# Second block's attention: two pipelines become one of 32 units, heads of the first kind taken in pairs, softmaxes mixed unscaled, and two chunks of the output projection moved beside it

## The chip, the cores and the metric

The kernel runs on one core of a Trainium2 chip. The metric is the device time of one execution in microseconds, from the program's start to its end on that core; lower is better.

## What is computed

`reference` runs two transformer blocks on 512 tokens of width 1024. The change touches only the attention of the second block. It has two kinds of heads. The first kind (`moba`) has 8 heads of width 64; with 512 tokens and blocks of 256 every query sees its own block and all earlier ones, so this is plain causal attention with a slope per head. The second kind (`diff`) has 4 heads with two query-key components of width 64 and values of width 128.

```
sc = q k^T * 64**-0.5 - slope * dist          # causal, both kinds
m_out = softmax(sc) v                          # first kind: 8 heads, v 64 wide
a = softmax(sc1) - lam * softmax(sc2)          # second kind: 4 heads
d_out = rms_norm(a v, diff_subln) * (1 - lambda_init)
mixed = concat(m_out * silu(mg), d_out * silu(dg))
x = x + mixed @ w_out
```

All of it is float32. The large products are made of three matmuls each, from a rounded high part and the low part that is left (`XAh`, `XAl` for the activations, `Rh`, `Rl` for the weights); the attention's own products are plain float32 matmuls.

## The kernel before

Everything is written by hand, engine by engine: five functions (`sync_program`, `tensor_program`, `scalar_program`, `gpsimd_program`, `vector_program`) issue each engine's instructions in order and wait on semaphores. `psum_plan` walks the same order and gives each use of one of the 8 PSUM banks its counts; `hold(tag)` waits until the bank's earlier use has been read. Weights come in 28 chunks of 128x1024 in the last part of the program (20 of `w_in2`, in groups `4, 5, 6, 3, 7` after the groups 0 to 2, and 8 of `w_out2`): SyncE loads one to `raw`, ScalarE writes its high part to a ring of five (`ahead`, L1079), GpSimd the low part (L1558), and TensorE runs 24 matmuls of 512 columns on it (`gemm_tok_chunk`, L652 to L654). This is called a chunk below.

`second_order` lays out the attention as a list of steps, `SECOND`, that every engine follows. A unit is one head and one block of 128 queries, which sees `nk` = 128, 256, 384 or 512 keys. For a unit, step A makes the scores (L1025), VectorE adds the slope (L2342), takes the maximum (L2346) and negates it (L2348), and ScalarE takes the exponential with its sum (L1508). Step B turns the softmax, `Pb`, with 1 to 4 transposes (L1037), which ScalarE copies to `PT2` (L1518). Step C multiplies it with v (L1054), and VectorE (L2359) or ScalarE (L1527) takes it to `mixed`. In a step n of the list C(n-3), B(n-2) and A(n) stand in a row, and then a piece of other work, `FILL_MOBA` or `FILL_DIFF`: chunks of the later projections, their norms (`norm2`), the transposes of q and k (`turn2`, L987), the gates.

The first kind is a pipeline of its own with 32 units, 36 steps and 12 chunks, the second another with 16 units, 19 steps that hold attention work and 8 chunks. A unit of the second kind has two halves of scores on two banks, and both softmaxes are scaled and added before the turning:

```
    own(e.tensor_scalar(p1, p1, s1[:, 3:4], None, ALU.mult))
    t = own(e.tensor_scalar(p2, p2, s2[:, 3:4], lam[:, 5:6], ALU.mult, ALU.mult))
    after(t)
    e.tensor_tensor(p1, p1, p2, ALU.add).then_inc(s["mixd"], 1)
```

After both pipelines follow the norm of the second kind's heads (L2385, with a square root by ScalarE), their gates (L2317), the 8 groups of four transposes of `mixed` (L1062), their high and low parts (L1540, L2392), the 8 chunks of the output projection, the addition of x (L2399) and the stores.

Of the kernel before, what the change touches and what calls it, by code (L numbers as in the profile page):

```python
# [94 lines left out]
for _m in range(NPARK):  # L95
    for _n in range(12):
        _k = 2 if 4 <= _n < 8 else 1
        if _m == NPARK // 2 and _n < 4:
# [7 lines left out]
FILL_MOBA = ([("proj", 4, 0), ("proj", 4, 1), ("proj", 4, 2), ("q2", 4, 2)]  # L106
             + [("proj", 5, 0, 2, 0), ("proj", 5, 1, 2, 1), ("proj", 5, 2, 2, 2), ("norm", 2, 3)]
             + [("turn", 2, k) for k in range(4)] + [("q2", 5, 3)]
             + [("proj", 6, 0, 3, 0), ("proj", 6, 1, 3, 1), ("proj", 6, 2, 3, 2), ("norm", 3, 3)]
             + [("turn", 3, k) for k in range(4)] + [("v2", 6, 1)])  # L110
FILL_DIFF = ([("proj", 3, 0), ("proj", 3, 1), ("proj", 3, 2), ("gate", 3, 0), ("gated", 0, 0), ("gated", 0, 2)]
             + [("proj", 7, 0), ("proj", 7, 1), ("proj", 7, 2), ("gate", 7, 1)])


def second_order():

    out = []
    for kind, units, fill, lag in (("m", 32, FILL_MOBA, 4), ("d", 16, FILL_DIFF, 7)):  # L120
        at = 0
        for n in range(units + lag):
            if kind == "d":
                for part in (2, 1, 0):
                    if n - 4 - part == 11 or (n - 4 - part == 15 and part < 2):
                        out.append(("dD", n - 4 - part, part))
            if 0 <= n - 3 < units:
                out.append((kind + "C", n - 3))
            if 0 <= n - 2 < units:
                out.append((kind + "B", n - 2))  # L130
            if n < units:
                out.append((kind + "A", n))
                steps = 22 if kind == "m" else 12
                take = (n + 1) * steps // units - n * steps // units
                out += fill[at:at + take]
                at += take
        out += fill[at:]
    return out
# [5 lines left out]
def psum_plan():  # L144
# [81 lines left out]
    n_ss = 0  # L226
    for step in SECOND:
# [6 lines left out]
        elif what in ("mA", "dA"):  # L234
            for i in range(1 if what == "mA" else 2):
                use(("ss", n_ss), n_ss % 2)
                n_ss += 1
        elif what in ("mB", "dB"):
            use(("tp", what[0], n), 2)
        elif what in ("mC", "dC"):  # L240
            use(("ap", what[0], n), 3)
    for k in range(8):
        use(("tm", k), (0, 1, 6, 7)[k % 4])
# [2250 lines left out]
```

## Time and profile before

| | us |
|---|---|
| median of 3 runs (lowest, highest) | 2395.33 (2394.08, 2401.38) |
| the profiled execution, its own time | 2386.53 |
| its span, first to last instruction | 2384.7 |
| TensorE busy in the span | 2175.2 (91%) |
| VectorE, GpSimd, ScalarE busy | 1780.5, 989.3, 944.7 |
| mean granted clock of TensorE | 0.951 |

The span is what the trace covers. A granted clock of 1.00 stands for TensorE's 2.4 GHz, 0.5 for its 1.2 GHz. The part that the change touches is the last 337 us of the span.

### The profile page before, as it was taken

The numbers are of one execution on the slowest core, as the hardware profiler recorded it, in microseconds if no ns is written. First come the engines' busy times: TensorE is split into PE (matmuls) and PEld (weight loads), VectorE is DVE, ScalarE is ACT, GpSimd is POOL, SyncE is SP. The second block draws the span as 40 slices with busy tenths as digits, with TensorE's granted clock in tenths as the row PEclk, the third lists the DMA queues.
The fourth block names the chain that finished last, engine by engine and source line by source line (L and its number), as shares of the span: only waits on it lengthen the run. The fifth ranks groups of instructions, "written<-read, shape, count | busy, mean of one in ns | idle before, by whom it ended". The sixth has DMA issues, their size and how long they took to land.

```text
span 2384.7 us, 29853 instructions
## 1 busy us (share of the span) xinstructions
PE 2175.2 (91%) x10645; PEld 1860.7 (78%) x10645; DVE 1780.5 (75%) x3593; ACT 944.7 (40%) x1543; POOL 989.3 (41%) x647
## 2 busy tenths in 40 slices
PE   3998899887899999899899999999999979998778
PEld 2786677666678999899788988889888867766557
DVE  7785887987553999999698788878888787444552
ACT  3335555434233444354333333333333343443441
POOL 2441122124353655699554345444444424311112
PEclk8999999998999999999999999999999999977779
DMA  7221111145542454366999999999999942211111
GB/s 292 76 89 59 57 58 63 63 158 176 194 168 81 162 167 149 119 238 240 328 362 370 347 335 342 357 338 358 333 345 361 340 161 102 71 36 36 36 36 45
DMA packets 176946, 455.84 MB, mean 191 GB/s; under 512 B 13600, under 2 KB 80544, under 8 KB 175136
## 3 DMA queue, kind: packets, MB, share of 16 engines
q1 hardware_dynamic: 136720, 293.55, 35.7%
q0 software_dynamic: 36864, 134.23, 15.0%
q10 hardware_dynamic: 3216, 26.15, 2.9%
q8 instruction: 86, 1.41, 0.2%
q14 instruction: 60, 0.49, 0.1%
HBM read 409.84 MB, written 44.04 MB: 190 GB/s over the span
## 4 chain that ended last, share of the span: by engine, by line
PE 63%; DVE 24%; ACT 4%; issue 2%; DMA 2%; POOL 0%; SPq 0%; ACTq 0%; DVEq 0%
PE bank L652 12%; PE bank L653 11%; PE bank L654 11%; PE bank L955 7%; PE bank L957 7%; PE bank L959 7%; DVE cout L1847 5%; DVE ohB L2130 4%; PE bank L1025 2%; DVE ohA L2129 2%; PE bank L1054 1%; DVE wk L2031 1%; DVE eqb L2081 1%; PE bank L1037 1%; DVE eqb L2077 1%
## 5 line engine op out<-in xcount | busy, mean ns | idle before, releaser
L1558 POOL TENSOR_TENSOR Rl<-raw,Rh 128x1024 fp32r<-128x1024 f32 x179 | 464.6, 2602 | 801.3 <-ACT Rh L1093 801.1
L652 PE MATMUL bank<-XAh,Rh 128*128 128x384 f32 (+1 forms) x1472 | 535.7, 364 | 37.2 <-POOL Rl L1558 15.4
L1093 ACT ACTIVATE Rh<-raw 128x1024 fp32r<-128x1024 f32 x380 | 399.6, 1056 | 352.6 <-DMA raw<-in_u 109.7
L653 PE MATMUL bank<-XAl,Rh 128*128 128x384 f32 (+1 forms) x1472 | 521.9, 355 | 0.0
L654 PE MATMUL bank<-XAh,Rl 128*128 128x384 f32 (+1 forms) x1472 | 521.8, 354 | 0.0
L652 PEld LDWEIGHTS bank<-XAh,Rh 128*128 128x128 f32 x1472 | 280.1, 190 | 60.5 <-issue 24.4
L653 PEld LDWEIGHTS bank<-XAl,Rh 128*128 128x128 f32 x1472 | 280.2, 190 | 18.3
L654 PEld LDWEIGHTS bank<-XAh,Rl 128*128 128x128 f32 x1472 | 279.5, 190 | 18.5
L1604 POOL DMA_INDIRECT ga<-in_v,eid x128 | 183.4, 1433 | 211.0 <-DVE y L2192 192.2
L1604 POOL DMA_INDIRECT ga<-in_un,eid x128 | 171.0, 1336 | 217.1 <-DVE act L2184 194.7
L955 PE MATMUL bank<-Rh,XGh 128*128 128x512 f32 x768 | 237.0, 390 | 2.6 <-issue 2.6
L957 PE MATMUL bank<-Rl,XGh 128*128 128x512 f32 x768 | 236.8, 389 | 0.0
L959 PE MATMUL bank<-Rh,XGl 128*128 128x512 f32 x768 | 236.7, 389 | 0.0
L2162 DVE TENSOR_TENSOR Rl<-raw,Rh 128x1024 fp32r<-128x1024 f32 x189 | 230.3, 1218 | 6.2 <-ACT Rh L1093 6.2
L1847 DVE SCALAR_TENSOR_TENSOR cout<-gb,vecs,cout 128x512 f32<-128x512 f32 x240 | 208.0, 866 | 2.1
L652 PE MATMUL bank<-Rh,XAh 128*128 128x512 f32 x416 | 172.2, 414 | 10.7 <-DVE XAl L1658 7.0
L2192 DVE SCALAR_TENSOR_TENSOR y<-ga,act,y 128x1024 f32<-128x1024 f32 x127 | 167.2, 1317 | 2.7
L955 PEld LDWEIGHTS bank<-Rh,XGh 128*128 128x128 f32 x768 | 143.8, 188 | 31.9 <-issue 2.9
L957 PEld LDWEIGHTS bank<-Rl,XGh 128*128 128x128 f32 x768 | 144.2, 188 | 30.2
L959 PEld LDWEIGHTS bank<-Rh,XGl 128*128 128x128 f32 x768 | 144.2, 188 | 30.1
L653 PE MATMUL bank<-Rl,XAh 128*128 128x512 f32 x416 | 167.6, 403 | 0.0
L654 PE MATMUL bank<-Rh,XAl 128*128 128x512 f32 x416 | 166.7, 401 | 0.0
(272 smaller groups left out, 3391.5 us busy)
## 6 DMA issues: line engine op xcount, KB each, us to landing
raw<-in_u SPq DMA_DIRECT2D x128, 512.0 KB, 8.1
raw<-in_v SPq DMA_DIRECT2D x128, 512.0 KB, 6.3
wd<-wb ACTq DMA_DIRECT2D x12, 2048.0 KB, 7.4
wg<-wd SPq DMA_DIRECT2D x30, 768.0 KB, 10.1
raw<-in_w_mod SPq DMA_DIRECT2D x32, 512.0 KB, 4.5
raw<-in_w_in SPq DMA_DIRECT2D x32, 512.0 KB, 3.6
gd<-pk SPq DMA_DIRECT2D x64, 192.0 KB, 1.9
gt<-gd SPq DMA_DIRECT2D x16, 768.0 KB, 11.0
```

Source lines behind the costliest of these rows:

```text
L652: e.matmul(o, sh, mh, start=first, stop=False)
L653: e.matmul(o, sh, ml, start=False, stop=False)
L654: return e.matmul(o, sl, mh, start=False, stop=last)
L955: e.matmul(o[i][:, :], XGh[:, x, tok], hi[:, 512 * i:512 * i + 512], start=first, stop=False)
L957: e.matmul(o[i][:, :], XGh[:, x, tok], lo[:, 512 * i:512 * i + 512], start=False, stop=False)
L959: t = e.matmul(o[i][:, :], XGl[:, x, tok], hi[:, 512 * i:512 * i + 512], start=False, stop=last)
L1093: e.activation(Rh[:, r % NRING, :], raw[:, n % NRAW, :], ACT.Copy).then_inc(s["hi"], 1)
L1558: e.tensor_tensor(Rl[:, r % NRING, :], raw[:, n % NRAW, :], Rh[:, r % NRING, :].bitcast(F32), ALU.subtract).then_inc(s["lo"], 1)
L1604: e.indirect_dma_start(ga[n % NGB][:, :], None, table[:, :], bass.IndirectOffsetOnAxis(ap=eid[:, n % 128:n % 128 + 1], axis=0)).then_inc(s ...
L1847: ins = e.scalar_tensor_tensor(out=o, in0=g[:, j:j + 512], scalar=vec("taps", 31 * cb + j), in1=o, op0=ALU.mult, op1=ALU.add)
L2162: e.tensor_tensor(Rl[:, r % NRING, :], raw[:, c % NRAW, :], Rh[:, r % NRING, :].bitcast(F32), ALU.subtract).then_inc(s["lov"], 1)
L2192: t = e.scalar_tensor_tensor(out=y0[:, :], in0=v, scalar=act0[:, j:j + 1], in1=y0[:, :], op0=ALU.mult, op1=ALU.add)
```

## The change

1. **One pipeline.** `second_order` makes 35 steps of 32 units: 16 of the first kind, then 16 of the second, with no drain between. `FILL` names for each step what stands behind its attention work. 20 steps hold a chunk of the projections, and steps 30 and 34 one of the output projection each. Steps 7, 12, 13, 15, 18, 21, 24, 27, 28, 29 and 31 to 33 hold none; 8 and 13 hold the four transposes of q's or k's blocks in one piece, 21 the first kind's gates, 27 the product of the second kind's gates and `diff_subln`, 28 the transposes of the first kind's half of `mixed`.
2. **Pairs.** A unit of the first kind is two heads that share 128 rows of q and k. Step A issues both halves, as in the second kind. Step B turns them one by one, the first ahead of A(n), the second behind it, both through bank 2. Step C makes two products side by side in one bank, and one VectorE instruction scales both. `Pb4` to `Pb7` move to free memory, since the first kind needs eight now.
3. **Mixing unscaled.** For the second kind P1 + c P2 is made, with c = -lam s1 / s2 by row, in one instruction. The factor 1 / s1 is applied by ScalarE when it takes the square and the copy out of the bank.
4. **Norm and gates.** The gates of the second kind are multiplied with `diff_subln` early (`gates_subln`), and norm, `diff_subln` and gate are then one instruction per head and block (`subln_head`), where there were two passes.
5. **Output projection.** `mixed` of the first kind is transposed in step 28 on banks 4 to 7, and the first two of its 8 chunks stand in steps 30 and 34. The last four groups of transposes follow the pipeline.

```diff
-    for kind, units, fill, lag in (("m", 32, FILL_MOBA, 4), ("d", 16, FILL_DIFF, 7)):
...
+    kinds = [("m", n) for n in range(16)] + [("d", n) for n in range(16)]
+    for n in range(35):
+        if n >= 3:
+            out.append((kinds[n - 3][0] + "C", kinds[n - 3][1]))
+        if 2 <= n < 34:
+            out.append((kinds[n - 2][0] + "B", kinds[n - 2][1], 0))
+        if n < 32:
+            out.append((kinds[n][0] + "A", kinds[n][1]))
+        if 2 <= n < 18:
+            out.append(("mB", n - 2, 1))
+        out += FILL.get(n, [])
...
+FILL = {0: [("proj", 4, 0)], 1: [("proj", 4, 1)], 2: [("proj", 4, 2)], 3: [("q2", 4)],
...
+        28: [("tm", k) for k in range(4)], 30: [("out", 0)], 34: [("out", 1)]}
```

TensorE, scores and products of the first kind:

```diff
-                        e.matmul(o[:, 0:nk], qk2[kind][p0:p0 + 64, hh // 2, qb * 128:(qb + 1) * 128],
-                                 qk2[kind + 1][p0:p0 + 64, hh // 2, 0:nk], start=True, stop=True).then_inc(done, 1)
+                        p0 = 64 * half
+                        e.matmul(o[:, 0:nk], qk2[kind][p0:p0 + 64, h, qb * 128:(qb + 1) * 128],
+                                 qk2[kind + 1][p0:p0 + 64, h, 0:nk], start=True, stop=True).then_inc(done, 1)
...
+                    for half in range(2):
+                        u = USES["tp", "m", n, half]
+                        e.wait_ge(free[u.bank], u.done)
+                        v0 = 128 * j + 64 * half
+                        for k in range(qb + 1):
+                            t = e.matmul(o[:, 64 * half:64 * half + 64], PT2[half][:, k, :], v2[0][:, k, v0:v0 + 64],
+                                         start=(k == 0), stop=(k == qb))
```

VectorE, mixing and norm:

```diff
-                    own(e.tensor_scalar(p1, p1, s1[:, 3:4], None, ALU.mult))
-                    t = own(e.tensor_scalar(p2, p2, s2[:, 3:4], lam[:, 5:6], ALU.mult, ALU.mult))
-                    after(t)
-                    e.tensor_tensor(p1, p1, p2, ALU.add).then_inc(s["mixd"], 1)
+                    t = own(e.reciprocal(st2[:, :, 3:4], st2[:, :, 2:3]))
+                    after(max(t, t_lam))
+                    t = own(e.tensor_scalar(st2[:, 1, 3:4], st2[:, 1, 3:4], st2[:, 0, 2:3], lam[:, 5:6],
+                                            ALU.mult, ALU.mult))
+                    after(t)
+                    e.scalar_tensor_tensor(out=Pb[i][:, 0:nk], in0=Pb[i + 1][:, 0:nk], scalar=st2[:, 1, 3:4],
+                                           in1=Pb[i][:, 0:nk], op0=ALU.mult, op1=ALU.add).then_inc(s["mixd"], 1)
...
+            def subln_head(h):
+                for b in range(4):
+                    o = mixed[:, b, 512 + h * 128:512 + (h + 1) * 128]
+                    e.scalar_tensor_tensor(out=o, in0=o, scalar=sml[:, 80 + 4 * h + b:81 + 4 * h + b],
+                                           in1=sg[1][:, b, h * 128:(h + 1) * 128], op0=ALU.mult, op1=ALU.mult
+                                           ).then_inc(s["gated"], 1)
```

How the order moves is seen at two places. The first is TensorE where q's second group is transposed, in the first kind. Before (L1054 product, L1037 turning of a softmax, L1025 scores, L987 transposes of q):

```order
L1037 MATMUL bank<-ident,Pb_193 128x128 x2
L1025 MATMUL bank<-qk_1_182,qk_0_181 128x512
L987 MATMUL bank<-ident,stg 128x128 x4
L1054 MATMUL bank<-v_0_188,PT_1_201 128x64 x2
L1037 MATMUL bank<-ident,Pb_194 128x128 x3
L1025 MATMUL bank<-qk_1_182,qk_0_181 128x128
L1054 MATMUL bank<-v_0_188,PT_0_200 128x64 x3
L1037 MATMUL bank<-ident,Pb_195 128x128 x4
L1025 MATMUL bank<-qk_1_182,qk_0_181 128x256
L987 MATMUL bank<-ident,stg 128x128 x4
L1054 MATMUL bank<-v_0_188,PT_1_201 128x64 x4
```

In the change (L1067 product, L1055 turning, L1042 scores, L988 transposes of q):

```order
L1067 MATMUL bank<-v_0_188,PT_0_200 128x64
L1067 MATMUL bank<-v_0_188,PT_1_201 128x64
L1055 MATMUL bank<-ident,Pb_194 128x128 x2
L1042 MATMUL bank<-qk_1_182,qk_0_181 128x512 x2
L1055 MATMUL bank<-ident,Pb_195 128x128 x2
L1067 MATMUL bank<-v_0_188,PT_0_200 128x64 x2
L1067 MATMUL bank<-v_0_188,PT_1_201 128x64 x2
L1055 MATMUL bank<-ident,Pb_196 128x128 x3
L1042 MATMUL bank<-qk_1_182,qk_0_181 128x128 x2
L1055 MATMUL bank<-ident,Pb_197 128x128 x3
L988 MATMUL bank<-ident,stg 128x128 x16
```

The scores go two heads at a time between the turnings of two halves, and the 16 transposes, which stood four by four behind single units, stand in one piece.

The second is VectorE in the second kind, from the mixing of a unit of 256 columns to that of the next. Before (L2366 to L2372 mix, L2342 to L2348 serve two halves of scores of the unit two further on):

```order
L2366 RECIPROCAL sml<-sml 128x1
L2367 RECIPROCAL sml<-sml 128x1
L2369 TENSOR_SCALAR Pb_194<-Pb_194,sml 128x256
L2370 TENSOR_SCALAR Pb_195<-Pb_195,sml 128x256
L2372 TENSOR_TENSOR Pb_194<-Pb_194,Pb_195 128x256
L2342 SCALAR_TENSOR_TENSOR Pb_198<-mrow,bank 128x512
L2346 TENSOR_REDUCE sml<-Pb_198 128x1
L2348 TENSOR_SCALAR sml<-sml 128x1
L2342 SCALAR_TENSOR_TENSOR Pb_199<-mrow,bank 128x512
L2346 TENSOR_REDUCE sml<-Pb_199 128x1
L2348 TENSOR_SCALAR sml<-sml 128x1
L2366 RECIPROCAL sml<-sml 128x1
L2367 RECIPROCAL sml<-sml 128x1
L2369 TENSOR_SCALAR Pb_196<-Pb_196,sml 128x384
L2370 TENSOR_SCALAR Pb_197<-Pb_197,sml 128x384
L2372 TENSOR_TENSOR Pb_196<-Pb_196,Pb_197 128x384
```

In the change (L2435 to L2440 mix, L2409 to L2415 serve the scores):

```order
L2435 RECIPROCAL sml<-sml 128x2
L2437 TENSOR_SCALAR sml<-sml 128x1
L2440 SCALAR_TENSOR_TENSOR Pb_194<-Pb_195,sml,Pb_194 128x256
L2409 SCALAR_TENSOR_TENSOR Pb_198<-mrow,bank 128x512
L2413 TENSOR_REDUCE sml<-Pb_198 128x1
L2415 TENSOR_SCALAR sml<-sml 128x1
L2409 SCALAR_TENSOR_TENSOR Pb_199<-mrow,bank 128x512
L2413 TENSOR_REDUCE sml<-Pb_199 128x1
L2415 TENSOR_SCALAR sml<-sml 128x1
L2361 TENSOR_TENSOR sg_204<-sg_204,rows 128x512 x4
L2435 RECIPROCAL sml<-sml 128x2
L2437 TENSOR_SCALAR sml<-sml 128x1
L2440 SCALAR_TENSOR_TENSOR Pb_196<-Pb_197,sml,Pb_196 128x384
```

Five instructions of a mixing, three of them as wide as the scores, are now three with one wide one; here the gates' product with `diff_subln` (L2361) stands between two mixings.

## Rows read from the trace of the kernel before

**Rows 1.** Timeline, TensorE, its first score matmul and its last matmul (start us, us, engine)

```profile
2047.49 0.70 PE L1025 MATMUL bank<-qk,qk 64*128 64x128 f32 x3
...
2381.10 0.39 PE L654 MATMUL bank<-Rh,XAl 128*128 128x512 f32 x1
```

**Rows 2.** Windows: each engine's busy us in a stretch, then TensorE's granted clock, DMA

```profile
2047.00:2334.00 287.00, 240.53 (x1020) 175.85 (x1019) 139.13 (x412) 124.67 (x294) 48.13 (x20) 0.81 0.13 39
2047.00:2102.00 55.00, 54.85 (x257) 41.79 (x255) 26.05 (x72) 24.06 (x48) 16.93 (x7) 1.00 0.23 68
2102.00:2138.00 36.00, 31.56 (x107) 21.81 (x107) 12.86 (x42) 12.74 (x31) 2.30 (x1) 0.57 0.05 15
```

**Rows 3.** Waits of TensorE, 2047 to 2338 us: total, times, longest

```profile
PE bank L1037 <- DVE Pb L2372: 27.8, 7, 7.2
PE bank L1037 <- ACT qk L1462: 7.4, 5, 2.0
PE bank L1062 <- DVE XAl L2392: 4.5, 1, 4.5
PE bank L1054 <- ACT PT L1518: 4.3, 8, 0.8
PE bank L1054 <- DVE mixed L2359: 1.9, 2, 1.7
```

**Rows 4.** Timeline, TensorE, high clock: turning, scores, product; a chunk's start, its end; second kind

```profile
2060.71 0.39 PE L1037 MATMUL bank<-ident,Pb 128*128 128x128 f32 x2
2061.03 1.12 PE L1025 MATMUL bank<-qk,qk 64*128 64x512 f32 x2
2062.08 0.66 PE L1054 MATMUL bank<-v,PT 128*128 128x64 f32 x4
2062.58 0.50 PE L1037 MATMUL bank<-ident,Pb 128*128 128x128 f32 x3
...
2079.91 0.50 PE L652 MATMUL bank<-Rh,XAh 128*128 128x512 f32 x1
...
2085.49 0.55 PE L1054 MATMUL bank<-v,PT 128*128 128x64 f32 x4
...
2223.47 1.13 PE L1025 MATMUL bank<-qk,qk 64*128 64x512 f32 x4
```

**Rows 5.** Timeline, TensorE: a chunk begun at the low clock, and what follows

```profile
2132.50 0.79 PE L652 MATMUL bank<-Rh,XAh 128*128 128x512 f32 x1
...
2140.15 0.33 PE L1054 MATMUL bank<-v,PT 128*128 128x64 f32 x2
```

**Rows 6.** Groups of instructions, VectorE, 2047 to 2385 us: busy us, mean ns, idle before

```profile
L2342 DVE SCALAR_TENSOR_TENSOR Pb<-mrow,bank 128x512 f32<-128x512 f32 x16 | 11.0, 688 | 25.6 <-PE bank L1025 25.5
...
L2346 DVE TENSOR_REDUCE sml<-Pb 128x1 f32<-128x512 f32 x16 | 11.0, 686 | 0.5
...
L2348 DVE TENSOR_SCALAR sml<-sml 128x1 f32<-128x1 f32 x64 | 9.8, 153 | 2.2
...
L2372 DVE TENSOR_TENSOR Pb<-Pb,Pb 128x512 f32<-128x512 f32 x4 | 2.8, 693 | 0.1
...
L2370 DVE TENSOR_SCALAR Pb<-Pb,sml 128x512 f32<-128x512 f32 x4 | 2.2, 541 | 0.0
```

**Rows 7.** Groups of instructions, ScalarE, the same stretch

```profile
L1508 ACT ACTIVATION_READ_ACCUMULATOR Pb<-Pb,sml 128x1 f32 x64 | 11.9, 187 | 0.0
...
L1508 ACT ACTIVATE Pb<-Pb,sml 128x512 f32<-128x512 f32 x16 | 11.6, 723 | 29.8 <-DVE sml L2348 29.8
...
L1518 ACT ACTIVATE PT<-bank 128x512 f32<-128x512 f32 x12 | 7.2, 597 | 18.5 <-PE bank L1037 18.4
```

**Rows 8.** Timeline: the square root for three heads' norms, and the turning that waited

```profile
2307.14 1.28 ACT L1097 ACT_TABLE_LOAD   x1
2308.43 0.21 ACT L1097 ACTIVATE sml<-sml 128x12 f32<-128x12 f32 x1
...
2311.53 0.66 PE L1037 MATMUL bank<-ident,Pb 128*128 128x128 f32 x2 [7.21 <-DVE Pb L2372]
```

More of the change, by code:

```diff
@@ L115, in second_order @@
 def second_order():
     out = []
-    for kind, units, fill, lag in (("m", 32, FILL_MOBA, 4), ("d", 16, FILL_DIFF, 7)):
[L121 to L137, printed above, removed]
@@ L141 @@
+    return out + [("dD", 3), ("dD", 4)]
 SECOND = second_order()
@@ L1038, in tensor_program @@
                     t.then_inc(done, 1)
-                elif what in ("mC", "dC"):
+                elif what == "mC":
+                    j, qb = n // 4, n % 4
+                    o, done = hold(("ap", "m", n))
+                    if n == 0:
+                        e.wait_ge(free[3], USES["pj", 2, 3].done)
+                    for half in range(2):
+                        u = USES["tp", "m", n, half]
+                        e.wait_ge(free[u.bank], u.done)
+                        v0 = 128 * j + 64 * half
+                        for k in range(qb + 1):
+                            t = e.matmul(o[:, 64 * half:64 * half + 64], PT2[half][:, k, :], v2[0][:, k, v0:v0 + 64],
+                                         start=(k == 0), stop=(k == qb))
+                    t.then_inc(done, 1)
+                elif what == "dC":
@@ L1058, in tensor_program @@
-            for k in range(8):
-                o, done = hold(("tm", k))
-                e.wait_ge(s["gated"], 4 if k < 4 else 8)
-                for tb in range(4):
-                    t = e.transpose(o[:, tb * 128:(tb + 1) * 128], mixed[:, tb, k * 128:(k + 1) * 128], ident[:, :])
-                t.then_inc(done, 1)
-            def mixed_ready(n, k):
-                u = USES["tm", k]
-                if n == 0:
-                    e.wait_ge(free[u.bank], u.done)
-            for g in range(2):
-                for q in range(4):
-                    gemm_tok_chunk(("w_out2", g, q), q, [("out", g, tb) for tb in range(4)],
-                                   [(XA, tb) for tb in range(4)], mixed_ready if g == 0 else None)
+                elif what == "tm":
+                    turned_mixed(n)
+                elif what == "out":
+                    out_chunk(0, n)
@@ L1077, in scalar_program @@
+            for k in range(4, 8):
+                turned_mixed(k)
+            for q in (2, 3):
+                out_chunk(0, q)
+            for q in range(4):
+                out_chunk(1, q)
         def scalar_program(e):
@@ L1535, in scalar_program @@
                         root("sub3", sml[:, 92:96])
-            for k in range(8):
-                u = USES["tm", k]
-                e.wait_ge(full[u.bank], u.full)
-                e.activation(XAh[:, k, :], bank[u.bank][:, :], ACT.Copy).then_inc(s["tmh"], 1)
+                elif what == "tm":
+                    mixed_high(n)
+                elif what == "out":
+                    ahead(CH["w_out2", 0, n] + 3)
+            for k in range(4, 8):
+                mixed_high(k)
             ahead(len(PLAN) - 1)
@@ L2349, in vector_program @@
                         n_ss += 1
[L2350 to L2353 removed]
+                elif what == "mB" and step[2] == 0:
+                    st2 = stats(n)
+                    e.wait_ge(s["pexp2"], 2 * n + 2)
+                    t_rc = own(e.reciprocal(st2[:, :, 3:4], st2[:, :, 2:3]))
                 elif what == "mC":
@@ L2381, in vector_program @@
-                    if n == 11 or part == 1:
-                        i = part if n == 11 else 3
-                        for b in range(4):
-                            o = mixed[:, b, 512 + i * 128:512 + (i + 1) * 128]
-                            t_dd = own(e.scalar_tensor_tensor(out=o, in0=o, scalar=sml[:, 80 + 4 * i + b:81 + 4 * i + b],
-                                                              in1=row("subln"), op0=ALU.mult, op1=ALU.mult))
-            after(t_dd)
-            gated(1, range(4))
@@ L2394, in vector_program @@
+            for k in range(4, 8):
+                mixed_low(k)
             e.wait_ge(s["xn"], 4)
```

231 lines of the change are left out of this document (135 added, 96 removed).

## The prediction

> **What bounds the kernel now.** I read the windows view first. The change touches nothing ahead of the first score matmul, which starts at 2047.49 us, and the last matmul of the program starts at 2381.10 [rows 1] and so ends by 2381.5: everything that can change lies in these 334.0 us. In the 287 us of attention TensorE is busy for 240.5 us, VectorE for 139.1, ScalarE for 124.7 and GpSimd for 48.1, and the granted clock averages 0.81 [rows 2]. So TensorE sets the pace, and no other engine is near full. It loses time in two ways. It waits: the waits view lists 27.8 us in 7 waits for the mixed softmax, 7.4 for the turned q and k, 4.5, 4.3 and 1.9 for others, together 45.9 us [rows 3]. And it is slow: from 2047 to 2102, with a chunk of projection behind almost every unit, its clock is 1.00 (2.4 GHz), and from 2102 to 2138, where it idled for 4.4 us between bare attention steps, 0.57, mostly the 1.2 GHz level [rows 2].
>
> To part the two I add up TensorE's work at the high level, start to start [rows 4]. A chunk of 24 matmuls takes 2085.49 - 2079.91 = 5.58 us, and 20 chunks of projection and 8 of output make 156.2. A score matmul of 512 columns takes 2062.08 - 2061.03 = 1.05; in proportion to columns the four sizes would average 0.66, and since a small one has its fixed part too I take 0.73: 48 groups, 35.0. Turning two blocks of a softmax takes 0.32 (2061.03 - 2060.71) and their product with v 0.50 (2062.58 - 2062.08); over sizes 1 to 4 I take 0.37 and 0.50, 48 of each, 41.8. Sixteen groups of four transposes of stg and mixed, at 0.47 (estimated as four of the turning step's), 7.5. Together 240.5. Then 334.0 - 240.5 - 45.9 = 47.6 us is the cost of the low clock and of small hand-offs. A chunk begun at the low level shows it: 2140.15 - 2132.50 = 7.65 us against 5.58 [rows 5]. Six chunks in the stretch begin so; at 1.5 us each, less than this one, they are 9 us, and the other 38 fall on attention steps without a chunk.
>
> **The change, term by term.**
>
> *Scores by pairs: -11.7 us.* The second kind already issues two halves, on rows 0 to 63 and 64 to 127 of the array, and the pair of 512 columns takes 1.13 us for 4 records where one head of the first kind takes 1.12 for 2 [rows 4]: the second half is free. The first kind has 32 single groups and will have 16 pairs: 16 x 0.73 = 11.7 us. Turns and products keep their number. TensorE's full-clock work falls to 228.8 us.
>
> *Mixing unscaled.* Before, a unit of 512 columns needs two reciprocals, two scalings (0.541 the dearer one) and an add (0.693) [rows 6], about 1.9 us on VectorE; now one reciprocal, one tiny product (0.153 for its kind) and one fused step, which I price at the 0.688 of the same form at the same width: 1.0 us. Over four sizes the gain averages 0.6 us per unit. It shortens only the path scores, maximum, mixing, turning, and only where TensorE waits there.
>
> *Fewer steps: the waits.* 36 + 19 steps of the pipelines become 35, and 22 of them hold a chunk (20 and two of the output), against 20 before. Where a chunk stands, its 5.58 us cover VectorE's 2 x (0.688 + 0.686 + 0.153) = 3.05 us for a pair, ScalarE's exponential (0.723 and 0.19 for its sum) and the copy (up to 0.597) [rows 6, 7]: 4.6 us, so I charge nothing. If that cover is gone the product of the unit three back waits 4.3 us (4.6, 0.3 for hand-offs, less the turning in between). Steps 7, 12, 13 and 15 of the first kind have none. Steps 7 and 15 hold 512 columns: 4.3 each. Step 12 holds 128 columns: 2.1. Step 8 and step 13 now turn all four blocks of q or k in one go through bank 2, each waiting for ScalarE's copy of the one before: 2 for the first, 3 x 0.8 after it (0.6 of copy, 0.2 of hand-offs), 4.5 a step, 9 against 7.4 before. That is 19.7 us. In the second kind steps 18, 21, 24, 27, 28, 29, 31 and 32 and the last one have none. Before, 7 such waits came to 27.8 [rows 3], 4.0 each; with 0.6 less mixing each, 9 x 3.4 = 30.6, of which I take 29, since the first of them begins with small units. In step 10 the square root between the units holds the copies back: 2. Sum 50.7 against 45.9: the waits do not fall, they are fewer and longer.
>
> The longest wait before, 7.21 us, was the square root's round trip with the norm's four products and the gates behind [rows 8]; the norm's gain now goes into the gates early (step 27, 2.7 us of VectorE in one lump, as the first kind's gates in step 21 are), and the roots fall into steps 31 and 34. Behind the last unit stands an output chunk of 5.6 us which covers square, root (1.28 + 0.21) and four products. So the 4.50 us wait of the turned `mixed` [rows 3] shrinks to about 0.8.
>
> *The low clock.* Attention work in steps without a chunk: before, 28 of the 48 units at 1.6 us, and 7.5 of transposes, 52 us, on which 38 us were lost. After, 4 pair steps of 2.5 us (0.73 + 2 x 0.37 + 2 x 0.50), 9 of 1.6 and 6 of transposes: 30 us. The same share of loss gives 22, and nine chunks will begin at the low level, 13.5. Together 35.5 against 47.6.
>
> *Elsewhere.* The queues of SyncE and GpSimd keep their order; weights come through five ring slots as before, and GpSimd's 48 us stay hidden. The output chunks begun early need `mixed` of the first kind only, done by step 21. ScalarE's square now reads the bank instead of `mixed`: 0.3 us either way.
>
> *Sum.* 228.8 + 50.7 + 35.5 = 315.0 us against 334.0: **-19 us**. A second count by steps, in which I followed TensorE, VectorE and ScalarE through all 35 steps with these durations, gave -21, so I take -20. The profiled execution took 2386.53 us (span 2384.7) and so would take 2366.5. The three runs shown have a median of 2395.33, 8.8 above it; the change is put on the median: 2375.3.
>
> **A rule weighed.** In the profile a load of ScalarE's tables takes 1.28 us, and the square root behind it starts at 2308.43, 0.01 after the load's end at 2307.14 + 1.28 [rows 8]. The sum uses 1.28. The Trainium skill, "ScalarE: Activation LUTs", section "What ACT_TABLE_LOAD costs", adds a drain of about 1.38 us to each switch, 2.66 in all. By that rule three switches that lie in the open here (steps 10, 21 and 31) would cost 4 us more, and the change would gain 16. The trace does not bear it out.
>
> **The rivals.**
>
> *The clock holds.* Steps 0 to 6 have a chunk each, and from 2047 to 2102 that kept the clock at 1.00 [rows 2]. If the remaining gaps are too few to lower it, the low clock costs 15 instead of 35.5: -40 us, 2355. Against it: before, single waits of 1.4 to 2.1 us were enough. Chance 0.14.
>
> *The pair's halves do not overlap in the first kind*, so that the change doesn't do what it says. The operands are laid out alike in both kinds, which speaks against it. Without the 11.7: -8 us, 2387. Chance 0.04.
>
> *Nothing gained.* The paths per step are twice as long in the first kind, and if every open step waits 5 us (13 x 5 = 65) and the clock stays low through them (40), the total is 334, as now: 2395. For it: VectorE's queue holds gates and norms ahead of the mixing. Chance 0.13.
>
> *Slower: bank 2 becomes the bound.* Both turned halves of a pair go through bank 2, and the second waits for ScalarE's copy of the first, which stands in ScalarE's queue behind evictions (4 x 0.6), a split (1.05) and roots. Where ScalarE is late by some 3 us in each of 16 pairs, that is 48 us, and -20 becomes +28: 2423. It decides from 27 / 16 = 1.7 us per pair on. Against it: ScalarE is busy for 124.7 of 287 us, and the scores between the two halves last 0.4 to 1.05 us, as long as the copy. Chance 0.06.
>
> *The forecast*, between -8 and -33: 0.63.
>
> **How the numbers follow.** Unknown are the waits (50.7; from 38, if two thirds of the second kind's open steps wait as the shorter ones did, to 63) and the low clock (15 to 47.6). Together these reach from -51 to +5; both ends at once are unlikely, and with 0.1 left out on each side the range is 2354 to 2391. What a measurement can tell from no change is 0.3%, 7 us. Faster by more: the forecast, the held clock and, just, the halves that don't overlap, 0.63 + 0.14 + 0.04 = 0.81. Slower by more: 0.06. Same: 0.13.
>
> **What would show it.** From the first score matmul to the last of the program: 314 us, not 334. Score matmuls of 512 columns in the first kind: 4 records in 1.13 us, 16 pairs. TensorE's waits: about 50 us, now on the products and turns of open steps, with those for the mixing some 30; the wait ahead of the turned `mixed` below 2 us. Granted clock 1.00 through steps 0 to 6, below 0.6 from step 7 to 8 and 12 to 14, and about 0.85 over the stretch. The forecast is wrong if the waits exceed 65 us, if the clock's average stays at 0.81, or if chunks in steps 0 to 6 have gaps ahead of them.

## The result and the profile after

| | before | after |
|---|---|---|
| median, us (lowest, highest) | 2394.70 (2393.36, 2401.38) | 2361.98 (2357.88, 2362.74) |
| the profiled execution, us | 2386.53 | 2357.88 |
| first score matmul to last matmul, us | 334.0 | 305.5 |
| TensorE's waits in that stretch, us | 46.5 | 44.0 |

The ratio of after to before is 0.9864, with an interval of 0.984 to 0.9888: faster by 32.7 us. Built and timed again beside a kernel before of its own, the change gave 0.9873 (0.9856 to 0.9891), 29.5 us. The forecast was 2375, 20 us less than before; the direction held, and 2361.98 lies within 2354 to 2391, 13 us below the forecast.

The comparisons below are made on "the stretch", from the first score matmul to the last matmul. "Waits" is the stretch less TensorE's busy time in it. An "open" step is one without a chunk, "turning" is the transposing of a softmax, and a "lump" is a run of VectorE instructions that stands in one piece. The windows view of the stretch, of the kernel before and of the changed one (us, busy us of PE, PEld, DVE, ACT, POOL, granted clock, DMA share, GB/s):

```profile
2047.49:2381.49 334.00, 287.52 (x1225) 215.20 (x1224) 148.28 (x425) 132.14 (x303) 60.07 (x25) 0.83 0.13 40
```

```profile
2047.31:2352.82 305.51, 261.54 (x1225) 201.29 (x1224) 137.66 (x361) 129.06 (x301) 59.51 (x25) 0.87 0.14 44
```

TensorE issues the same 1225 matmuls, yet is busy for 26 us less: the first kind's scores now run two heads at a time, and the granted clock rises from 0.83 to 0.87. The stretch is 28.5 us shorter, of which only 2.5 are waits. By place, the same view of the changed kernel:

```profile
2047.00:2103.00 56.00, 53.98 (x276) 41.77 (x274) 30.75 (x80) 26.93 (x58) 16.63 (x7) 1.00 0.25 75
2103.00:2123.00 20.00, 14.22 (x57) 10.68 (x57) 3.50 (x12) 8.43 (x18) 2.38 (x1) 0.66 0.08 28
2123.00:2151.00 28.00, 26.75 (x151) 21.22 (x150) 21.07 (x50) 13.05 (x26) 7.12 (x3) 1.00 0.13 40
2151.00:2175.00 24.00, 18.27 (x74) 13.51 (x74) 6.96 (x22) 9.29 (x23) 0.02 (x1) 0.64 0.07 21
2272.00:2294.00 22.00, 14.57 (x59) 11.07 (x60) 14.78 (x40) 10.73 (x33) 0.00 (x0) 0.61 0.01 2
```

Where one step with a chunk follows another the clock is 1.00 (2.4 GHz). The low places lie behind open steps: step 8 behind 7 (2103 to 2123), 13 and 14 behind 12 and 13 (2151 to 2175), and 28 to the start of step 30's chunk (2272 to 2294). TensorE's waits in the changed kernel, 2047 to 2353 us (total, times, longest), which answer to [rows 3]:

```profile
PE bank L1055 <- DVE Pb L2440: 20.7, 8, 4.6
PE bank L1067 <- ACT PT L1547: 8.3, 3, 3.6
PE bank L988 <- ACT qk L1480: 4.7, 6, 0.8
PE bank L1078 <- ACT PT L1547: 4.5, 5, 1.5
PE bank L988 <- ACT PT L1547: 3.9, 2, 2.2
PE bank L1055 <- ACT PT L1547: 1.4, 3, 1.0
PE bank L653 <- DVE XAl L2367: 0.2, 1, 0.2
```

The turning still waits for the mixing (27.8 before, 20.7 now); new are 8.3 us ahead of products of the first kind, behind the open steps 7, 12 and 15. The 4.50 us of before stood ahead of the transposes of the second kind's half of `mixed`, as TensorE's timeline of the kernel before shows:

```profile
2333.80 3.67 PE L1062 MATMUL bank<-ident,mixed 128*128 128x128 f32 x16 [4.50 <-DVE XAl L2392]
```

Those transposes now wait for nothing, and 0.20 us are left ahead of the chunk behind them. The timeline of TensorE, changed kernel: a pair of 512 columns in step 3; steps 7 and 8; an output chunk in the tail with the last turned `mixed` behind it.

```profile
2067.02 1.13 PE L1042 MATMUL bank<-qk,qk 64*128 64x512 f32 x4
...
2104.76 0.66 PE L1067 MATMUL bank<-v,PT 128*128 128x64 f32 x4 [3.56 <-ACT PT L1547]
2105.26 0.62 PE L1055 MATMUL bank<-ident,Pb 128*128 128x128 f32 x3
2105.81 0.80 PE L1042 MATMUL bank<-qk,qk 64*128 64x128 f32 x4
2106.54 0.90 PE L1055 MATMUL bank<-ident,Pb 128*128 128x128 f32 x3
2109.12 1.12 PE L988 MATMUL bank<-ident,stg 128*128 128x128 f32 x4 [1.68 <-ACT PT L1547]
2111.01 1.11 PE L988 MATMUL bank<-ident,stg 128*128 128x128 f32 x4 [0.78 <-ACT qk L1480]
...
2310.94 0.77 PE L653 MATMUL bank<-Rh,XAh 128*128 128x512 f32 x1
...
2317.82 1.91 PE L1009 MATMUL bank<-ident,mixed 128*128 128x128 f32 x16
2319.93 0.47 PE L653 MATMUL bank<-Rh,XAh 128*128 128x512 f32 x1 [0.20 <-DVE XAl L2367]
```

Four records in 1.13 us: the pair's second half is free. Behind the wait of 3.56 us the same kind of turning, three blocks, takes 0.62 and then 0.90 where it took 0.50 before [rows 4], the first of a run of work at the low level. The chunk from 2310.94 to 2317.82 takes 6.88 against 5.58, because it too begins low: its first matmuls take 0.63 us each, the later ones 0.39.

What holds the product of step 8 for 3.56 us is seen on ScalarE, changed kernel:

```profile
2102.10 0.72 ACT L1532 ACTIVATE Pb<-Pb,sml 128x512 f32<-128x512 f32 x1 [2.30 <-DVE sml L2415]
...
2103.62 0.72 ACT L1532 ACTIVATE Pb<-Pb,sml 128x512 f32<-128x512 f32 x1 [0.70 <-DVE sml L2415]
...
2104.34 0.36 ACT L1547 ACTIVATE PT<-bank 128x256 f32<-128x256 f32 x1
```

The second half of the pair is turned by 2100.8, but its copy stands in ScalarE's queue behind the two exponentials of step 7, and these wait for VectorE's slope, maximum and negation of both halves.

VectorE's mixing of 512 columns, groups view of the changed kernel (busy us, mean ns, idle before; all sizes for the two small ones):

```profile
L2437 DVE TENSOR_SCALAR sml<-sml 128x1 f32<-128x1 f32 x16 | 4.4, 273 | 0.6
L2440 DVE SCALAR_TENSOR_TENSOR Pb<-Pb,sml,Pb 128x512 f32<-128x512 f32 x4 | 3.0, 752 | 0.1
L2435 DVE RECIPROCAL sml<-sml 128x2 f32<-128x2 f32 x16 | 2.6, 163 | 0.0
```

That is 1.19 us, where 1.0 was forecast; the same sum of means was 2.0 before. The small product with two operands takes 0.273 where 0.153 was put down for it, and the wide step 0.752 where 0.688 was.

### The profile page after: what moved, and what is told of

Read it like the earlier page. It is cut to its first block, busy times and chain, and to the rows that moved or that the text cites. A ratio compares the mean times of both kernels' runs of the same rounds, so it can differ in the third digit from the quotient of the medians.

```text
span 2356.0 us, 29765 instructions
## 1 busy us (share of the span) xinstructions
PE 2148.9 (91%) x10645; PEld 1845.8 (78%) x10645; DVE 1762.5 (75%) x3529; ACT 942.5 (40%) x1541; POOL 984.9 (42%) x647
## 4 chain that ended last, share of the span: by engine, by line
PE 61%; DVE 25%; ACT 4%; issue 3%; DMA 2%; POOL 0%; SPq 0%; ACTq 0%; DVEq 0%; POOLq 0%
PE bank L653 12%; PE bank L654 11%; PE bank L655 11%; PE bank L956 7%; PE bank L958 7%; PE bank L960 7%; DVE cout L1880 5%; DVE ohB L2163 4%; DVE ohA L2162 2%; PE bank L1042 1%; DVE wk L2064 1%; DVE eqb L2114 1%; DVE eqb L2110 1%; PE bank L1055 1%; PE bank L1067 1%
```

## The experiments

Each is the changed kernel with one edit, or with several where it says so. The "stretch" figures compare with 305.5 us. The changed kernel run once more (e12) gave 305.6, of which 44.7 are waits and 260.9 busy time against 44.0 and 261.5; so a stretch is read to about 1 us, and a split into waits and busy time no finer. The medians of e2, e3, e4, e5, e6, e8 and e10 rest on two executions each and can't tell parts of a few us apart.

**e1, the pair's halves kept apart.** A small matmul over the full height of the array stands between the halves of the first kind; it writes 32 columns that the half behind it overwrites.

```diff
+                        if half and kind == 0:
+                            e.matmul(o[:, 0:32], ident[:, :], ident[:, 0:32], start=True, stop=True)
```

> The change, with one small matmul over all 128 rows (32 columns) between the two halves of scores of each of the 16 pairs of the first kind. The stretch from the first score matmul to the end of the last matmul is 305.5 us in the change and 334.0 before. Theory 1, the pairs are cheap because their halves run at the same time on two groups of rows: the 4 records of a pair of 512 columns take about 2.2 us in place of 1.13, the sixteen pairs cost 16 x (0.73 + 0.1) = 13 us more, and the stretch is 315 to 319 us, since nearly all pairs stand on TensorE's own path. Rival, what counts is the smaller number of steps, and the score time lies in waits that are there anyway: under 4 us more.

Ratio to before 0.9927 (0.9903 to 0.9951), 2376.2 us; stretch 315.5, +10.0. TensorE's timeline:

```profile
2073.08 1.12 PE L1044 MATMUL bank<-qk,qk 64*128 64x512 f32 x2
2074.13 0.41 PE L1043 MATMUL bank<-ident 128*128 128x32 f32 x2
2074.47 1.12 PE L1044 MATMUL bank<-qk,qk 64*128 64x512 f32 x2
```

The pair now lasts 2.5 us (2075.6 - 2073.1), and the rival's "under 4 us more" is out. Busy time rose by 15.8 us and the waits fell by 5.9, since a longer step covers more of them. Of the 10 us, the extra matmuls are up to 16 x 0.34 = 5.4 start to start, so this bounds the worth of overlapping the halves, with the other parts in place, between about 5 and 10. That is below the 11.7 of its term, which did not count the waits that it opens.

**e2, the mixing as wide as before**, with three wide instructions and the same number of small ones.

```diff
-                    e.scalar_tensor_tensor(out=Pb[i][:, 0:nk], in0=Pb[i + 1][:, 0:nk], scalar=st2[:, 1, 3:4],
-                                           in1=Pb[i][:, 0:nk], op0=ALU.mult, op1=ALU.add).then_inc(s["mixd"], 1)
+                    p1, p2 = Pb[i][:, 0:nk], Pb[i + 1][:, 0:nk]
+                    own(e.tensor_scalar(p1, p1, 1.0, None, ALU.mult))
+                    t = own(e.tensor_scalar(p2, p2, st2[:, 1, 3:4], None, ALU.mult))
+                    after(t)
+                    e.tensor_tensor(p1, p1, p2, ALU.add).then_inc(s["mixd"], 1)
```

> The change, with the mixing of the second kind made again of three wide VectorE instructions (a product of P1 with 1, one of P2 with the factor, an add), the small ones as in the change. Each unit's mixing is 0.29 to 0.49 plus 0.34 to 0.54 us longer. Theory 1, TensorE's 8 waits for the mixing (20.7 us) lie at the end of a path through it: each grows by about 0.8 us, the waits by 5 to 7 and the stretch of 305.5 us by 6 to 10 with what the low clock adds. Rival, VectorE has room and ScalarE's exponentials end the wait: below 2 us.

0.9877 (0.9789 to 0.9966), 2367.3 us; stretch 312.7, +7.2, waits +6.4. The row of the waits view:

```profile
PE bank L1055 <- DVE Pb L2444: 27.5, 9, 5.2
```

27.5 against 20.7, while VectorE is busy for 9.0 us more: three quarters of the mixing's added time come back in TensorE's waits. As theory 1 had it.

**e3, the whole output projection behind the attention.**

```diff
-        28: [("tm", k) for k in range(4)], 30: [("out", 0)], 34: [("out", 1)]}
+        28: [("tm", k) for k in range(4)]}
...
```

> The change, with both early chunks of the output projection taken out of steps 30 and 34 and put behind the pipeline again; the transposes of the first kind's half of mixed stay in step 28. Theory 1, the two chunks cover about 4 us of paths each and keep the clock up: two more waits of 3 to 4 us (step 31's mixing; the last head's norm ahead of the last four transposes), 2 to 4 us of low clock, so the stretch grows by 8 to 13 us from 305.5. Rival, those paths are covered by the units themselves, and moving 11 us of work is neutral: within 3 us.

0.9872 (0.9776 to 0.9969), 2366.1 us; stretch only 306.8, +1.3: theory 1's 8 to 13 failed, and the rival's "within 3" came out, though not for its reason. The waits rose by 4.8 (the mixing's from 20.7 to 25.2, with a new one of 3.0 in step 31), but TensorE was busy for 3.5 us less: all 8 chunks stand in one run at 1.00, where the two early ones take 6.7 and 6.9. The cover is real and mostly paid back by the clock. The other wait that theory 1 named, ahead of the last transposes, did not come.

**e4, two pipelines again**, 38 steps, each kind with its own filling and draining.

```diff
-    kinds = [("m", n) for n in range(16)] + [("d", n) for n in range(16)]
-    for n in range(35):
+    for kind in ("m", "d"):
+        for n in range(19):
...
```

> The change, with the 32 units again in two pipelines with a drain between them (38 steps for 35); pairs, mixing, chunks and output as in the change. Theory 1, a drain costs the waits of three more steps without a chunk (the last two units of the first kind and the first of the second with nothing beside them): 4 to 9 us on 305.5. Rival, the single pipeline is the heart of the change, as most of the steps went with it: 15 us or more.

0.9879 (0.9767 to 0.9991), 2367.7 us; stretch 309.4, +3.9, just under the 4 to 9 of theory 1; waits +2.5, busy time +1.4. The rival's 15 us and more are out: by itself the single pipeline is a small part of the gain.

**e8, norm and gates in two passes**, the product of gates and `diff_subln` in step 27 gone, the gates multiplied behind the last head's norm.

```diff
...
-                    e.scalar_tensor_tensor(out=o, in0=o, scalar=sml[:, 80 + 4 * h + b:81 + 4 * h + b],
-                                           in1=sg[1][:, b, h * 128:(h + 1) * 128], op0=ALU.mult, op1=ALU.mult
-                                           ).then_inc(s["gated"], 1)
+                    t = own(e.scalar_tensor_tensor(out=o, in0=o, scalar=sml[:, 80 + 4 * h + b:81 + 4 * h + b],
+                                                   in1=row("subln"), op0=ALU.mult, op1=ALU.mult))
...
-                        subln_head(3)
+                        after(subln_head(3))
+                        gated2()
```

> The change, with norm, gain and gate of the second kind in two passes as before: 16 products with the gain by head, then four of 512 columns with the gates ahead of the last transposes; nothing in step 27. Theory 1, the 2.7 us of VectorE in step 27 and the four gates at the end both lie on paths: step 27's wait of 4.6 us falls by 2 to 3 with its low clock, and at the end 2.7 us and the transposes' wait come back, so the stretch changes by -1 to +5. Rival, the single pass is what was left unexplained of the 28.5 us (the other parts, taken back one by one, gave 10.0, 7.2, 1.3 and 3.9, together 22.4): +6.

0.9866 (0.9837 to 0.9895), 2359.5 us; stretch 302.6, -2.9, outside the -1 to +5 expected, a miss. TensorE's timeline behind step 27, first the changed kernel, then e8:

```profile
2276.50 0.87 PE L1055 MATMUL bank<-ident,Pb 128*128 128x128 f32 x3 [4.55 <-DVE Pb L2440]
```

```profile
2278.15 0.88 PE L1055 MATMUL bank<-ident,Pb 128*128 128x128 f32 x3 [2.15 <-DVE Pb L2447]
```

This wait fell by 2.4 us as expected; what was wrong is the end, where two passes were to cost 2.7 us and a wait, and the transposes wait 1.04. In the changed kernel the single pass costs a little: the output chunk behind the last unit covers two passes nearly as well, and the lump of step 27 stands ahead of a mixing.

**e9, the edits of e1, e2, e3, e4 and e8 together.**

> The change with five parts taken back at once: halves of scores kept apart, three wide instructions for the mixing, output projection behind, two pipelines, norm in two passes. What is left of it is that the first kind has 16 steps with two heads each in place of 32 with one. Taken back one by one the five moved the stretch from 305.5 us by 10.0, 7.2, 1.3, 3.9 and -2.9, together 19.5, to 325.0, and 334.0 was before. Theory 1, they add, and the 9.0 us left are the halved number of steps: 322 to 328. Rival, the parts lean on each other through the clock (a part alone is worth less while the others hold the clock up): 331 to 337, and the number of steps is worth nothing.

0.9987 (0.9975 to 0.9998), 2390.7 us against 2393.0; stretch 334.2, as the kernel before's 334.0. One by one the five edits cost 10.0 + 7.2 + 1.3 + 3.9 - 2.9 = 19.5; together 28.7. Theory 1's 322 to 328 failed, and the stretch lies where the rival had it. Windows view of the stretch, then TensorE's timeline and waits ahead of the transposes of the second kind's half of `mixed`:

```profile
2054.61:2388.82 334.21, 286.04 (x1257) 217.45 (x1256) 145.45 (x393) 130.24 (x301) 59.96 (x25) 0.85 0.13 40
...
2341.67 1.73 PE L1010 MATMUL bank<-ident,mixed 128*128 128x128 f32 x7 [5.00 <-DVE mixed L2372]
```

This wait of 5.00 us is absent in e3 and 1.0 in e8: without the early output chunk and with two passes, nothing covers the end of the norm. So two of the parts stand in for each other at this place. But the waits as a whole don't make the 9.2 us that are left over. One by one the five moved them by -5.9, +6.4, +4.8, +2.5 and -0.9, together +7.0; at once they rise by 4.2, to 48.2. The busy time moved by 15.8, 0.8, -3.5, 1.4 and -2.0, together 12.5; at once it rises by 24.5. So the surplus is 12 us of busy time, for the same matmuls as in e1, at a lower clock (0.85 against 0.87 or 0.88 in each of the five alone): the parts lean on each other through the clock, as the rival said. Which of them together lower it stays open.

The kernel still has its units in pairs and so 38 steps instead of 55, and yet the time of before. That does not show that fewer steps are worth nothing: besides the 5.4 us or less of e1's small matmuls, e9 keeps the transposes of q and k in one piece, which cost (see e6), and the transposes in step 28. What the number of steps earns by itself no run here parts out.

**e5, the clock held up.** At ten steps of the list, in or behind open ones, TensorE runs 3 to 12 more matmuls of 512 columns ahead of a product or a turning, 71 in all (the 3 of step 18 go twice, ahead of its product and of its turning), on the bank that the next scores overwrite. Nothing reads them.

```diff
+WARM = {8: 10, 13: 3, 16: 10, 18: 3, 19: 9, 22: 12, 25: 3, 28: 12, 29: 3, 30: 3}
...
+            def warm(count):
+                o, done = hold(("ss", n_ss))
+                for i in range(count):
+                    e.matmul(o[:, :], XAh[:, 4, 0:128], XAh[:, 4, :], start=True, stop=True)
```

> The change, with 3 to 12 extra matmuls of 512 columns (0.23 us each at the high clock) ahead of the attention work of ten steps that follow a step without a chunk; they write a bank of scores that has been read and is about to be written, and nobody reads what they leave. Of the 305.5 us, TensorE's waits are 44.0 and about 33 us are low clock and hand-offs. Theory 1, the low clock follows from the waits and costs on its own: filling the waits keeps the granted clock near 1.00 behind steps 7, 15, 18, 21 and 27, and the stretch shrinks by 8 to 18 us although 70 matmuls are added. Rival, the paths through VectorE and ScalarE bound the open steps whatever the clock: the extra matmuls delay each product by what they overrun and the stretch is 305 to 312.

0.9841 (0.9806 to 0.9877), 2353.7 us; stretch 294.8, -10.7. Windows view of the stretch, and TensorE's timeline in steps 7 and 8:

```profile
2057.99:2352.81 294.82, 264.82 (x1296) 205.39 (x1295) 137.65 (x361) 128.97 (x301) 59.49 (x25) 0.94 0.15 45
...
2111.89 2.58 PE L1027 MATMUL bank<-XAh 128*128 128x512 f32 x10 [0.40 <-DVE Pb L2422]
...
2115.43 0.66 PE L1080 MATMUL bank<-v,PT 128*128 128x64 f32 x4 [0.57 <-ACT PT L1560]
2115.93 0.50 PE L1068 MATMUL bank<-ident,Pb 128*128 128x128 f32 x3
2116.36 0.49 PE L1055 MATMUL bank<-qk,qk 64*128 64x128 f32 x4
```

The product of step 8 starts 57.44 us into the stretch; in the changed kernel it was 57.45, behind a wait of 3.56. The filling delays nothing here, and the turning and the scores behind it take 0.50 and 0.49 where they took 0.62 and 0.80. Over the stretch the waits fell from 44.0 to 30.0. The 71 matmuls are worth about 16.3 us (an estimate, 71 x 0.23), so they more than use up those 14.0; the other work took 248.5 us where it took 261.5, and that is the gain. TensorE has more to do and is done earlier.

**e6, the turns of q and k inside the next chunk.** One group of four transposes stands behind each block's wait of the chunk of v; v's last chunk moves from step 14 to 13.

```diff
...
+                        gemm_tok_chunk(("w_in2", n, 3), 3, [("pj", n, tb) for tb in range(4)],
+                                       [(XA, tb) for tb in range(4)],
+                                       lambda tb, k: turn2(n - 3, tb) if k == 6 else None)
...
```

> The change, with the four transposes of q (step 8) and of k (step 13) no longer in one piece ahead of a chunk: each group of four stands ahead of a quarter of the chunk (6 matmuls, 1.4 us), for which that of step 14 moves to step 13 and step 14 has none. Theory 1, the 8.6 us of waits at those transposes (1.68, 2.21 and 6 of 0.78) go, since 1.4 us of matmuls cover ScalarE's 0.6 us copy, and with them the low clock of about 6 us of transposes; step 14 without a chunk costs one wait of 2 to 3 us back: the stretch is 8 to 14 us shorter than 305.5. Rival, the wait moves to the next turning of a softmax and the open step 14 gives the rest back: within 4 us.

0.985 (0.9819 to 0.9881), 2355.8 us; stretch 298.1, -7.4. The six waits of 0.78 us are gone; the first of each group stays, as TensorE's timeline shows:

```profile
2116.87 1.09 PE L988 MATMUL bank<-ident,stg 128*128 128x128 f32 x4 [1.72 <-issue]
```

and step 14, now open, adds one of 3.14. That is why it fell just short of the 8 expected. The windows view of the stretch shows where the gain lies:

```profile
2054.92:2352.99 298.07, 253.67 (x1225) 196.93 (x1224) 137.60 (x361) 127.87 (x301) 59.50 (x25) 0.90 0.15 45
```

The waits as a whole are 44.4, as before the edit. The same 1225 matmuls are busy for 7.9 us less, at 0.90: what the transposes in one piece cost was the clock.

**e7, e5 and e6 together**, and six matmuls more in step 15, since e6 leaves step 14 open.

```diff
+WARM = {8: 10, 13: 3, 15: 6, 16: 10, 18: 3, 19: 9, 22: 12, 25: 3, 28: 12, 29: 3, 30: 3}
...
```

> Both together: the transposes inside chunks and the extra matmuls in steps behind an open one. Theory 1, the two gains add, for they lie at different steps: stretch 275 to 290 us, time of one execution 15 to 30 us below the change. Rival, each alone already lets the clock recover and together they give no more than the better one.

0.981 (0.9784 to 0.9836), 2347.8 us against 2392.6 before; stretch 288.0 at a clock of 0.96. -17.5, where the two alone give -10.7 and -7.4: they add up. The rival, no more than the better one, is out. The time is 44.8 us below the kernel before, and with e11, from which it can't be told apart, it is the fastest found.

**e10, VectorE's lumps moved.** The gates of step 21 go behind step 22's chunk, the product of step 27 behind step 30's.

```diff
-        16: [("proj", 3, 0)], 17: [("proj", 3, 1)], 19: [("proj", 3, 2)], 20: [("gate", 3, 0)], 21: [("gated", 0)],
-        22: [("proj", 7, 0)], 23: [("proj", 7, 1)], 25: [("proj", 7, 2)], 26: [("gate", 7, 1)], 27: [("subg", 7)],
-        28: [("tm", k) for k in range(4)], 30: [("out", 0)], 34: [("out", 1)]}
+        16: [("proj", 3, 0)], 17: [("proj", 3, 1)], 19: [("proj", 3, 2)], 20: [("gate", 3, 0)],
+        22: [("proj", 7, 0), ("gated", 0)], 23: [("proj", 7, 1)], 25: [("proj", 7, 2)], 26: [("gate", 7, 1)],
+        28: [("tm", k) for k in range(4)], 30: [("out", 0), ("subg", 7)], 34: [("out", 1)]}
```

> The change, with two lumps of VectorE work (four products of 512 columns each, 2.7 us) moved from a step without a chunk into one with: the first kind's gates from step 21 to 22, the product of gates and gain from step 27 to 30. Theory 1, the lump is the largest part of the waits of 3.97 and 4.55 us behind steps 21 and 27; each falls by 2 to 2.7 us, part of its low clock goes too, and nothing comes back, since a chunk covers 5.7 us: the stretch is 299 to 302. Rival, it only moves: step 31's mixing then waits for the lump of step 30: 304 to 307.

0.9876 (0.9849 to 0.9903), 2363.8 us; stretch 304.4, -1.1, a miss; the rival's 304 to 307 came out. TensorE's timeline, first the changed kernel, then e10:

```profile
2233.22 0.45 PE L1055 MATMUL bank<-ident,Pb 128*128 128x128 f32 x1 [3.97 <-DVE Pb L2440]
```

```profile
2235.84 0.30 PE L1055 MATMUL bank<-ident,Pb 128*128 128x128 f32 x1 [1.57 <-DVE Pb L2440]
...
2245.43 0.41 PE L1055 MATMUL bank<-ident,Pb 128*128 128x128 f32 x2 [0.98 <-DVE Pb L2440]
```

The wait of 3.97 became 1.57, and a new one of 0.98 stands ahead of the next turning, behind the moved gates. The one behind step 27 fell from 4.55 to 2.14, as theory 1 had it; in step 31, which the rival named, no wait came, and the one in step 32 stayed at 3.8. All in all the waits fell by 3.1 us, busy time rose by 2.1, and the clock stayed at 0.87: theory 1's "nothing comes back" and the recovered clock are what failed.

**e11, e5, e6 and e10 together**, with the counts of e7 but for steps 22 and 28 (4 in place of 12, since the waits there are shorter) and 29 (6 in place of 3).

> Transposes inside chunks, lumps moved, and extra matmuls in the steps behind an open one (fewer where the lump is gone). Theory 1, the gains add: 288.0 us with the first and third, and 3 to 5 less with the lumps, although with the clock up a lump is worth only its wait: 283 to 286, one execution 15 to 22 us below the change. Rival, with the clock up the lumps are worth nothing more: 287 to 289.

0.9816 (0.9792 to 0.984), 2350.0 us; stretch 288.4 against 288.0 of e7, the rival's 287 to 289: with these counts the moved lumps are worth nothing more.

**e12, the changed kernel once more**, beside the runs of e9 to e11.

> The changed kernel itself, once more, beside the others on one chip. Both theories: the stretch again within 0.5 us of 305.5, so that differences of over 1 us between stretches mean something; the whole time may differ by some 5 us from run to run, which would then lie ahead of the stretch.

2363.4 us; stretch 305.6 against 305.5, windows view:

```profile
2061.21:2366.83 305.62, 260.92 (x1225) 201.16 (x1224) 137.66 (x361) 129.04 (x301) 59.59 (x25) 0.87 0.14 44
```

Its profiled span is 14 us longer than the first one (2370.0 against 2356.0), and its first score matmul is 13.9 us later: that spread lies ahead of everything the change touches. In this one repeat the stretch came within 0.1 us, and it is the better measure for differences of a few us.

## Why the prediction was right, and where its sizes were off

**TensorE sets the pace: held.** GpSimd and ScalarE are busy for 59 to 61 and 128 to 130 us in every run of the changed kernel and its variants, less than half of the stretch, whatever its length. VectorE counts where its work stands ahead of a turning (e2).

**Scores by pairs, -11.7: the mechanism held, its size is only bounded.** 1.13 us for four records; the pairs of the four sizes take 0.42, 0.64, 0.85 and 1.06 us start to start in steps 0 to 3, 0.74 on average against the 0.73 of the sum. So TensorE is rid of the 11.7 us, but by e1 the stretch is shorter by at most 10 of them. The rival of halves that do not overlap is out.

**Mixing unscaled: held, and it counts for more than its place in the sum.** 1.19 us instead of 1.0 for 512 columns, the small product with two operands mis-sized most, and 7.2 us in e2, which leaves the reciprocals and the small product as they are.

**The waits, 50.7: too high, 44.0 measured.** This is the largest error of the sum, and here the sign was wrong too: they were to rise by 4.8 and fell by 2.5. The open steps 7 and 15 wait 3.56 instead of 4.3, step 12 1.2 instead of 2.1, the transposes of q and k 8.6 instead of 9: 16.9 against 19.7. The path through VectorE, the exponential and the copy was read rightly. In the second kind 20.7 and 4.5 make 25.2 against 29. Behind step 10, with the root, 1.0 instead of 2. The estimate of 3.4 us per open step was the flaw: it came from the mean of 4.0 of the seven waits of before [rows 3], and one of these is the 7.21 us of the square root's round trip, which the prediction itself takes away in its next paragraph. The other six make 20.6 us, 3.4 each; with 0.6 less for the mixing, nine of 2.8 are 25. The text said "fewer and longer"; [rows 3] list 23 waits and the rows of after 28: they are more, and shorter.

**The low clock, 35.5: 32.7.** It is what is left of 305.5 after 228.8 and 44.0, and 228.8 is the prediction's own sum, so an error in that would stand here; no view shows the term by itself. Average 0.87 against "about 0.85". Steps 0 to 6 ran at 1.00 as said; behind steps 7 and 12 it was 0.66 and 0.64, not below 0.6. Against the held clock the prediction put single waits of 1.4 to 2.1 us. The first fall of before comes with one of 1.75 us (ahead of 2106.53; the clock is 1.00 ahead of it, and 0.50 from 2106.5 to 2112), and in the changed kernel one comes behind a wait of 1.18 (ahead of 2152.70; 1.00 before it, 0.68 from there to 2158), while the wait of 1.03 ahead of 2142.67 was followed by none. The rival of the held clock was not what happened, but e5 shows that it was there to be had: 10.7 us of it with matmuls that compute nothing.

**The tail, 4.50 to 0.8: nothing ahead of the transposes, 0.20 behind them.** Right, but e3 and e8 show that either of two parts alone nearly does it (no wait in e3, 1.04 in e8); only with both taken back (e9) do 5.00 us return. "Output chunk covers square, root and products" and "one pass" are two covers of one wait.

**The norm's early lump: read as neutral, it costs.** e8 gains 2.9 us without it.

**Nothing gained, and slower through bank 2: out.** The open steps wait less than 5 us, 3.4 on average (44.0 over 13), and the turnings of softmaxes wait for ScalarE's copies 1.4 us in all, where that rival needed 1.7 us per pair. But the path that it named is there: the 8.3 us ahead of products and 3.9 ahead of the first transposes of q and k are waits for the copy of a pair's second half, which stands behind the exponentials in ScalarE's queue. Together these are 12.2 of the 44.0 us. No run here issues that copy earlier, so what the order costs is not shown.

**The sum.** The gain was 32.7 us where 20 were forecast, and the range held. 315.0 (314 with the second count) against 305.5: 7 us of waits and 3 of clock. The other 4 us of the 13 lie outside: I put 8.8 us between the profiled execution and the median, and here that is 4.1.

**The rule weighed.** ScalarE's timeline in the changed kernel, at a switch of tables:

```profile
2271.14 1.28 ACT L1532 ACT_TABLE_LOAD   x1
2272.43 0.72 ACT L1532 ACTIVATE Pb<-Pb,sml 128x512 f32<-128x512 f32 x1
```

The exponential starts 0.01 us after the load's end (2271.14 + 1.28), and the copy ahead of the load ends at 2271.12. The drain of the Trainium skill ("ScalarE: Activation LUTs", section "What ACT_TABLE_LOAD costs") did not show here either; the trace's 1.28 was the figure to use.

## What to carry to other kernels

Where an engine waits and is slow at once, price the two together: a wait costs its own length and what the clock takes from the work behind it, and filling it with matmuls that nobody reads gave 10.7 us here. Issue two half-height products of 64 rows side by side where they exist; here that was worth 5 to 10 us. Take changes back one at a time and all together: the difference (19.5 against 28.7) shows that parts cover for each other, and splitting it into waits and busy time shows how. When a price is the mean of some waits, leave out those that the change takes away.

## What the runs showed of the hardware

- The granted clock rose from 0.87 to 0.94 with 71 more matmuls, and the work of the stretch ended 10.7 us earlier.
- With transposes moved inside chunks (e6) the waits stayed at 44 us and the same matmuls were busy for 7.9 us less, at 0.90.
- Two matmul groups on rows 0 to 63 and 64 to 127 run together (1.13 us for 512 columns each); one matmul of 32 columns over all 128 rows between them makes it 2.5.
- VectorE's product with two scalar operands on a 128x1 column takes 273 ns, where one with a constant took 153 [rows 6]. Its fused step of 512 columns takes 752 ns with a factor by row (L2440) and 685 with a constant (L2409).
